# Three HGRN projections cut by halves of the heads, the query taken token-major, and the recurrence two slots earlier, in a one-core hybrid encoder block

## What is computed

```python
proj = h @ w_in[l]
(q_hg, i_hg, f_fw, f_bw, g_hg, c_q, c_kv, k_rope, q_mem, gates) = _split(proj, IN_SPLITS)

q = heads(jax.nn.silu(q_raw)); v = heads(i_raw)
f = lbz + (1.0 - lbz) * jax.nn.sigmoid(f_raw)      # forward and backward
k = heads(1.0 - f); log_f = heads(jnp.log(f))
o = _chunk_gla(qz, kz, vz, gz)                     # S_t = diag(f_t) S_{t-1} + k_t v_t^T ; o_t = S_t^T q_t
o = _rmsnorm(o[0] + flip(o[1]), norm_g) * jax.nn.sigmoid(g_raw)
```

## Time and profile before

| | us |
|---|---|
| median of 3 runs | 1706.37 (1706.21 to 1706.91) |
| the profiled execution | 1706.24 |
| its span | 1704.5 |
| PE busy | 1699.0 |
| DVE busy | 1168.3 |
| ACT busy | 815.7 |
| POOL busy | 94.1 |

### The profile page before, as it was taken

How to read it: one execution, slowest core, us unless ns; L and a number is a source line. 1 busy time by engine, 2 the same in 40 slices (tenths; PEclk the granted TensorE clock), 3 DMA queues, 4 the chain that set the end, 5 groups by cost and what they waited for, 6 DMA issues and landing times.

```text
span 1704.5 us, 20450 instructions
## 1 busy us (share of the span) xinstructions
PE 1699.0 (100%) x8694; PEld 1411.7 (83%) x8694; DVE 1168.3 (69%) x1024; ACT 815.7 (48%) x674; POOL 94.1 (6%) x87
## 2 busy tenths in 40 slices
PE   9999999999999999999999999999999999999999
PEld 8888888898888888888888888888888888888886
DVE  4854566678877655545666679888989798655445
ACT  4454445454545445444444526554554555443332
POOL 0000002222222100000000000000000000000000
PEclk9999999999999999999999999999999999999999
DMA  9676776455665687667888958778787876878553
GB/s 363 240 251 209 253 242 210 174 172 184 184 208 197 198 248 270 214 213 252 256 269 278 360 198 255 242 230 260 237 243 252 240 236 180 261 239 306 198 197 124
DMA packets 137370, 397.98 MB, mean 233 GB/s; under 512 B 22336, under 2 KB 51392, under 8 KB 122816
## 3 DMA queue, kind: packets, MB, share of 16 engines
q1 hardware_dynamic: 129568, 377.15, 66.0%
q0 software_dynamic: 2720, 10.49, 3.3%
q10 hardware_dynamic: 4992, 9.05, 1.4%
HBM read 365.06 MB, written 30.93 MB: 232 GB/s over the span
## 4 chain that ended last, share of the span: by engine, by line
PE 99%; DVE 0%; ACT 0%; issue 0%; POOL 0%; DVEq 0%; POOLq 0%
PE pair L2145 21%; PE pair L2146 21%; PE pair L2147 21%; PE pair L2417 4%; PE pair L2415 4%; PE pair L2416 4%; PE pair L2119 3%; PE side L2397 3%; PE side L2395 3%; PE side L2396 3%; PE pair L2117 1%; PE pair L2397 1%; PE pair L2396 1%; PE pair L2395 1%; PE side L2227 1%; PE pair L2129 1%
## 5 line engine op out<-in xcount | busy, mean ns | idle before, releaser
L1396 DVE TENSOR_TENSOR weight_lo<-raw,weight_hi 128x2048 fp32r<-128x2048 f32 x210 | 481.0, 2292 | 396.2 <-ACT weight_hi L974 393.6
L974 ACT ACTIVATE weight_hi<-raw 128x2048 fp32r<-128x2048 f32 x210 | 402.3, 1916 | 520.1 <-DMA raw<-in_stream 519.9
L2145 PE MATMUL pair<-weight_hi,act_both 128*128 128x512 f32 x928 | 368.5, 397 | 0.6 <-DVE weight_lo L1396 0.6
L2147 PE MATMUL pair<-weight_hi,act_both 128*128 128x512 f32 x928 | 361.6, 390 | 0.0
L2146 PE MATMUL pair<-weight_lo,act_both 128*128 128x512 f32 x928 | 361.4, 389 | 0.0
L2145 PEld LDWEIGHTS pair<-weight_hi,act_both 128*128 128x128 f32 x928 | 174.3, 188 | 37.0 <-issue 1.0
L2147 PEld LDWEIGHTS pair<-weight_hi,act_both 128*128 128x128 f32 x928 | 174.2, 188 | 36.7
L2146 PEld LDWEIGHTS pair<-weight_lo,act_both 128*128 128x128 f32 x928 | 174.3, 188 | 35.3
L1295 ACT ACTIVATE part_hi<-part_raw 128x2048 fp32r<-128x2048 f32 x60 | 113.7, 1912 | 123.6 <-DVE part_raw L1887 49.8
L1867 DVE TENSOR_TENSOR part_lo<-part_raw,part_hi 128x2048 fp32r<-128x2048 f32 x60 | 136.4, 2281 | 42.7 <-ACT part_hi L1295 42.6
L2145 PE MATMUL pair<-weight_hi,ff_both 128*128 128x512 f32 x352 | 136.9, 389 | 0.0
(11 more groups left out here) (320 smaller groups left out, 2546.4 us busy)
## 6 DMA issues: line engine op xcount, KB each, us to landing
raw<-in_stream SPq DMA_DIRECT2D x256, 1024.0 KB, 5.5
part_raw<-in_stream SPq DMA_DIRECT2D x30, 1024.0 KB, 6.9
part_raw<-in_stream POOLq DMA_DIRECT2D x10, 1024.0 KB, 10.7
scratch<-spill ACTq DMA_DIRECT2D x32, 256.0 KB, 5.1
ln_rows<-in_ln_rows SPq DMA_DIRECT2D x6, 1024.0 KB, 8.3
gate<-scratch SPq DMA_DIRECT2D x12, 512.0 KB, 6.9
ff_scratch<-ff_blocks SPq DMA_DIRECT2D x11, 512.0 KB, 6.6
ff_land<-ff_scratch SPq DMA_DIRECT2D x44, 128.0 KB, 5.5
```

The costliest lines, as they stand in the source:

```text
L974: act.activation(hi_of(n), raw_of(n), ACT.Copy).then_inc(extra_h if extra(n) else h_ready, 1)
L1396: dve.tensor_tensor(lo_of(n), raw_of(n), hi_of(n).bitcast(F32), ALU.subtract)\
L2145: pe.matmul(out, hi[:, k0 + k, tok], w_hi[:, k, :], start=first and k == 0, stop=False)
L2147: mm = pe.matmul(out, lo[:, k0 + k, tok], w_hi[:, k, :], start=False, stop=last and k == 3)
```

## The change

The pieces of `f_fw`, `f_bw` and `q_hg` are cut by halves of the heads and put in the order f_fw0, f_bw0, q_hg0, f_fw1, f_bw1, q_hg1, four pieces each, in the same 24 slots (24 to 47). The query's pieces become token-major, like the gates', with the same way through transposition, DRAM and `f_land`; silu is applied where the gates have the sigmoid. `HG_SLOT` goes from 49 to 47. All other phases keep their slots; so do the first 8 attention units, while the 4 memory units, which are counted from the end of the recurrence, come two slots earlier.

```diff
-PHASES = [("mem_k", 8), ("mem_v", 8), ("c_q", 4), ("c_kv", 4), ("f_fw", 8), ("f_bw", 8), ("q_hg", 8), ("i_hg", 8),
+PHASES = [("mem_k", 8), ("mem_v", 8), ("c_q", 4), ("c_kv", 4), ("f_fw0", 4), ("f_bw0", 4), ("q_hg0", 4),
+          ("f_fw1", 4), ("f_bw1", 4), ("q_hg1", 4), ("i_hg", 8),
...
+HG_ROWS = ("f_fw", "f_bw", "q_hg")
+HG_HALVES = [(_name, _c) for _c in range(2) for _name in HG_ROWS]
...
-SPLIT = ("mem_k", "q_hg")
+SPLIT = ("mem_k",)
...
-TURNED = [(_name, _c) for _name in ("f_fw", "f_bw", "q_mem", "g_hg") for _c in range(2)]
-TURNED_TAKEN = [FIRST[_name] + 4 * (_c + 1) for _name, _c in TURNED]
+TURNED = HG_HALVES + [(_name, _c) for _name in ("q_mem", "g_hg") for _c in range(2)]
+TURNED_TAKEN = [FIRST[f"{_name}{_c}"] + 4 for _name, _c in HG_HALVES]\
+    + [FIRST[_name] + 4 * (_c + 1) for _name, _c in TURNED[len(HG_HALVES):]]
...
-F_ROWS = 4
+F_ROWS = len(HG_HALVES)
...
-HG_SLOT, HG_STEPS, PAIRS = FIRST["i_hg"] + 1, 12, 4
+HG_SLOT, HG_STEPS, PAIRS = FIRST["i_hg"] - 1, 12, 4
...
                 if n - 6 in TURNED_TAKEN[:F_ROWS]:
                     i = TURNED_TAKEN.index(n - 6)
-                    f, c = (f_fw, f_bw)[i // 2], i % 2
+                    c, d = divmod(i, 3)
+                    to = (f_fw, f_bw, q_hg)[d]
...
-                    act.activation(squared(f[:, 4 * c:4 * c + 4, :]), slices(f_land[:, i % 2]), ACT.Sigmoid)\
-                       .then_inc(f_open, 1)
-                j = n - 1 - FIRST["q_hg"]
-                if 2 <= j <= 8 and j % 2 == 0:
-                    wait_taken(act, GROUP["q_hg"] + j // 2 - 1)
-                    act.activation(q_hg[:, j - 2:j, :], q_hg[:, j - 2:j, :], ACT.Silu).then_inc(q_open, 1)
+                    act.activation(squared(to[:, 4 * c:4 * c + 4, :]), slices(f_land[:, i % 2]),
+                                   ACT.Silu if d == 2 else ACT.Sigmoid).then_inc(f_open, 1)
...
                 if s == 0:
-                    if p == 0:
-                        dve.wait_ge(q_open, 4)
-                        dve.wait_ge(f_done, F_ROWS)
+                    if p % 2 == 0:
+                        dve.wait_ge(f_open, 3 * (p // 2 + 1))
+                        dve.wait_ge(f_done, 2 * (p // 2 + 1))
...
-                j = n - FIRST["q_hg"]
-                if 2 <= j <= 8 and j % 2 == 0:
-                    add_halves(n, GROUP["q_hg"] + j // 2 - 1, q_hg[:, j - 2:j, :])
...
-            t_phase("f_fw", 8, 4, act_hi, act_lo)
-            t_phase("f_bw", 8, 4, act_hi, act_lo)
-            f_phase("q_hg", 8, act_both)
+            for name, c in HG_HALVES:
+                t_phase(f"{name}{c}", 4, 4, act_hi, act_lo)
```

More of the change, by code:

```diff
@@ L66 @@
     PIECES += _count
-GROUPS = {"mem_k": 4, "mem_v": 2, "q_mem": 2, "g_hg": 2, "f_fw": 2, "f_bw": 2, "q_hg": 4, "i_hg": 2, "c_q": 1, "c_kv": 1,
+GROUPS = {"mem_k": 4, "mem_v": 2, "q_mem": 2, "g_hg": 2, "f_fw0": 1, "f_bw0": 1, "q_hg0": 1,
+          "f_fw1": 1, "f_bw1": 1, "q_hg1": 1, "i_hg": 2, "c_q": 1, "c_kv": 1,
           "uq_nope": 4, "uq_rope": 2, "uk": 4, "uv": 2, "k_rope": 1, "gates": 12, "branch": 12, "w_o": 4, "ffn": 2,
@@ L75 @@
     _g += GROUPS[_name]
-TWO_BY_256 = ("c_q", "c_kv", "f_fw", "f_bw", "q_mem", "g_hg", "gates", "branch", "ffn")
-SPLIT = ("mem_k", "q_hg")
+HG_ROWS = ("f_fw", "f_bw", "q_hg")
+HG_HALVES = [(_name, _c) for _c in range(2) for _name in HG_ROWS]
+TWO_BY_256 = ("c_q", "c_kv") + tuple(f"{_name}{_c}" for _name, _c in HG_HALVES)\
+    + ("q_mem", "g_hg", "gates", "branch", "ffn")
+SPLIT = ("mem_k",)
 LOW = {}
@@ L86 @@
 U_KM, U_VM, U_GATES = 0, 4, 8
-TURNED = [(_name, _c) for _name in ("f_fw", "f_bw", "q_mem", "g_hg") for _c in range(2)]
-TURNED_TAKEN = [FIRST[_name] + 4 * (_c + 1) for _name, _c in TURNED]
+TURNED = HG_HALVES + [(_name, _c) for _name in ("q_mem", "g_hg") for _c in range(2)]
+TURNED_TAKEN = [FIRST[f"{_name}{_c}"] + 4 for _name, _c in HG_HALVES]\
+    + [FIRST[_name] + 4 * (_c + 1) for _name, _c in TURNED[len(HG_HALVES):]]
+TURNED_GROUP = [GROUP[f"{_name}{_c}"] for _name, _c in HG_HALVES]\
+    + [GROUP[_name] + _c for _name, _c in TURNED[len(HG_HALVES):]]
 TURNED_SAVED = [_n + 5 for _n in TURNED_TAKEN]
 TURNED_FETCHED = [_n + 7 for _n in TURNED_TAKEN]
-F_ROWS = 4
+F_ROWS = len(HG_HALVES)
 LOOK = 2
@@ L344, in encoder_program @@
         f_open = sem("f_open")
-        q_open = sem("q_open")
         f_done = sem("f_done")
@@ L553, in columns_of_two @@
                             src = phase(name, "(c h b f) p e -> c b f p h e", h=2, b=3, f=2)[c, b, q // 2]
-                        elif name in ("f_fw", "f_bw", "q_mem", "g_hg"):
+                        elif name[:-1] in HG_ROWS:
+                            first = FIRST["f_fw0"] + 8 * HG_ROWS.index(name[:-1])
+                            src = stream[first:first + 8].rearrange("(c h f) p e -> c f p h e", h=2, f=2)
+                            src, q = src[int(name[-1]), j // 2], j
+                        elif name in ("q_mem", "g_hg"):
                             c, q = j // 4, j % 4
@@ L1103, in slot @@
                         act.wait_ge(kz_done, 1)
-                    take(n, GROUP[name] + c, rows[:], ACT.Copy, 512)
+                    take(n, TURNED_GROUP[i], rows[:], ACT.Copy, 512)
                 if n - 6 in TURNED_TAKEN[:F_ROWS]:
                     i = TURNED_TAKEN.index(n - 6)
-                    f, c = (f_fw, f_bw)[i // 2], i % 2
+                    c, d = divmod(i, 3)
+                    to = (f_fw, f_bw, q_hg)[d]
                     if i == 0:
@@ L1667, in slot @@
                     name, c = TURNED[i]
-                    wait_taken(dve, GROUP[name] + c)
+                    wait_taken(dve, TURNED_GROUP[i])
                     rows, blocks = (f_rows, f_blocks[:]) if i < F_ROWS else (qg_rows, qg_blocks[:])
@@ L1673, in slot @@
                         squares(blocks, t, rows[:, t, :], rows_blocked)
-                if n - 7 in TURNED_TAKEN[:F_ROWS]:
-                    i = TURNED_TAKEN.index(n - 7)
-                    d, c = divmod(i, 2)
+                i = TURNED_TAKEN.index(n - 7) if n - 7 in TURNED_TAKEN[:F_ROWS] else None
+                if i is not None and TURNED[i][0] != "q_hg":
+                    c, d = divmod(i, 3)
                     f = (f_fw, f_bw)[d]
```

## The result

The changed kernel takes **1712.99 us** (median of 8 runs, 1709.69 to 1714.01) against 1706.36 (median of 8, 1705.94 to 1707.20): a ratio of 1.0035 with a 95% interval of 1.0025 to 1.0044. It is slower by 6.6 us, where 1707.5 was forecast with a range of 1704.9 to 1709.1. The profiled execution is the slowest of the eight: 1714.01 us with a span of 1712.2, 7.8 us more than the one before.

A forecast was written before the change was run, and what follows sets the result against it. PE alone was taken to set the time. 1706.24 - 1.03 for the query + 2.15 for the passage gave 1707.36; with the median 0.13 higher, 1707.5 us was forecast, range 1704.9 to 1709.1.

The forecast's parts named there:

- What bounds the kernel: Whole kernel: PE alone sets the time, busy 1699.0 us of 1704.5; only PE's own work or new PE waits count.
- The query's form, -1.03: Eight query pieces: token-major form needs 64 matmuls fewer on PE, 1.03 us less, all on the path.
- the query saves nothing: Rival at the query pieces: the token-major form saves nothing, with the stall in place, 1708.5 us; chance 0.04.
- What is exchanged beside PE, 0: DVE, ACT and SP exchanges hidden by PE's 5.44 us pieces; PE's side products cost 0, between -0.3 and +0.3.
- The passage from pair 0 to pair 1, +2.15 between 1.65 and 2.55: Pieces 60 to 62: PE late for step 1 through DVE's late hg_rs reading, containing 1.05 us for piece 61's bank.
- The recorded reading of rows 7 and 8: DVE's query rotation: one of two equal multiplications took 2.06 us beside a POOL instruction, the other 1.22.
- The other passages: Slots 72 and 84: PE has more time and slot 72 no rotation, so no stall should decide there.
- The rival named 1711.8: The passage costs 2.15 us at all three pairs, slots 72 and 84 too; 0.10 with any other large stall.
- all passages or another large stall: Line of the chances: stalls at all three pair passages or some other large stall, 1711.8 us; chance 0.10.
- In most slots nothing: Recurrence two slots earlier: costs nothing in most slots, except at the passage from one pair of heads to the next.

The follow-up runs named there:

- experiment 2: Changed kernel with the recurrence put back to its old slot (49), leaving the order by halves and the token-major query: 1706.02 us against 1706.72 for the kernel before.
- experiment 6, first kernel: Changed kernel with the qm_land fetches behind loads 104 and 105 and DVE's query rotation in slot 62 instead of 60: 1706.52 us, ratio 0.9999.
- experiment 1: Changed kernel with the eight qm_land fetches put back behind weight loads 104 and 105: 1707.66 us against 1706.72 for the kernel before, ratio 1.0005.
- one copy: Changed kernel with fetches put back, rotation in slot 62, later step 1 packing, plus one unused ACT copy ahead of piece 104's split: 1706.68 us.
- experiment 6: Three kernels on the changed one with fetches put back: rotation in slot 62, 1706.52 us; step 1 packing behind k_nope's second taking (the 2.24 stall), 1708.01; both, 1705.83.
- experiment 7: Changed kernel with rotation in slot 62 and later step 1 packing, but the qm_land fetches left ahead of load 104: 1711.44 us against 1706.54 before.
- experiment 6 with both edits: Changed kernel with fetches behind loads 104 and 105, rotation in slot 62 and step 1 packing behind k_nope's second taking: 1705.83 us, ratio 0.9995.

## Why the prediction was wrong, point by point

- **What bounds the kernel.** Right: apart from the start and the 1.03 us of matmuls saved, all of the difference between the two traces is PE kept waiting or PE at a lower clock.
- **The query's form, -1.03.** Right. The first matmuls of pieces 32, 40 and 48 are now at 189.44, 232.96 and 276.48: 43.52 us for either eight, the figure that the earlier trace rows gives for the token-major ones. The rival "the query saves nothing" falls.
- **What is exchanged beside PE, 0.** Right as to DVE and ACT: experiment 2 shows no new wait beside the pieces that were exchanged; its one new wait, 0.3 us at 923.58, is far behind them.
- **The passage from pair 0 to pair 1, +2.15 between 1.65 and 2.55.** Right in place, order and size, and 0.27 too high. The timeline of DVE in the changed kernel answers to the earlier trace rows:

```profile
356.38 1.22 DVE L1493 TENSOR_TENSOR rope_x<-rope_x,cos 128x1024 f32<-128x1024 f32 x1
357.51 1.45 DVE L1494 TENSOR_TENSOR rope_swapped<-rope_swapped,sin 128x1024 f32<-128x1024 f32 x1
358.99 1.32 DVE L1496 SCALAR_TENSOR_TENSOR q_rope<-rope_swapped,small,rope_x 128x1024 f32<-128x1024 f32 x1
...
364.44 0.68 DVE L1568 TENSOR_SCALAR hg_rs<-side 128x512 f32<-128x512 f32 x1
```

  and that of PE to the earlier trace rows:

```profile
356.91 0.40 PE L2252 MATMUL side<-square_lo,ones_hi 128*128 128x512 f32 x1
357.24 0.46 PE L2232 MATMUL side<-q_hat,k_hat 128*32 128x32 f32 x32
358.70 0.50 PE L2150 MATMUL pair<-weight_hi,c_hi 128*128 128x512 f32 x1 [1.01 <-ACT k_nope L1017]
...
365.18 0.46 PE L2232 MATMUL side<-q_hat,k_hat 128*32 128x32 f32 x32 [0.72 <-DVE hg_rs L1568]
```

  With L = 357.31 the rotation begins at L - 0.93 (forecast L - 0.9), the reading ends at L + 7.81 (L + 7.6 to 8.5), piece 61 waits 1.01 (1.05), and step 1 starts at L + 7.87 instead of L + 5.99: 1.88 late. (The recorded sum is itself off by 0.05: the middle of 1.65 and 2.55 is 2.10, with a tenth for the signal 2.20.) About half of the excess is the rotation, 3.93 us (356.38 to 360.31) instead of the middle of 3.6 and 4.5, 4.05: beside POOL's copies its second operation took 1.45, where it had taken 2.06 beside POOL's multiplication. The rest is in terms of a few hundredths each, such as the signal, 0.06 and not 0.1.
  The recorded reading of rows 7 and 8 is too simple: POOL's record, 355.10 to 356.96, lies beside both multiplications nearly equally long, and only the second one is longer. What the rotation takes without POOL is shown by experiment 6, first kernel, where POOL's last copy ends as the rotation begins: 1.21, 1.22 and 1.28, 3.67 in all (forecast 3.6). Its second operation there:

```profile
370.30 1.22 DVE L1494 TENSOR_TENSOR rope_swapped<-rope_swapped,sin 128x1024 f32<-128x1024 f32 x1
```

- **The other passages.** Right that they don't decide: no wait of PE is seen at slots 72 and 84. The rival named 1711.8 for it, near the measured time, but by a mechanism that did not happen. The line of chances widens it to "all passages or another large stall" with 0.10; that is what came, but no place and no cause was named for it, so the nearness of 1711.8 to 1712.99 is luck. A number that fits is no support for its story.
- **The step that failed** is "In most slots nothing, since a product of the recurrence has a whole slot between its packing and its use". It looks at the products only. The edit moves everything that is counted from `HG_END`, and on SP that includes the eight `qm_land` fetches, past two loads that are not moved, 104 and 105; `prob_t` is queued behind the first. The prediction names SP once, for the savings that were added and their fetches, and never asks what the two slots carry past on its queue. The term that it lacked is 3.47 us in the profiled execution (experiment 1 takes away 5.3 by the medians, the clock's part included), and its danger could have been read before: 0.72 us between the end of `prob_t` and PE, behind a split that had waited 4.82 us for its load, and fetches that take SP 3.79 us to issue.
- **The second omission** is the clock. All of the sum's stalls were priced at their own length. That holds for the passage, where the stalls were short, and not behind piece 102, where 2.75 us came on top of 3.47.

With both terms, taken from the slowest execution, and the measured passage the sum by the prediction's own method would have been 1706.37 - 1.03 + 1.88 + 3.47 + 2.75 = 1713.4; measured 1712.99.

## What to carry to other kernels

When an edit changes a number that other places count from, list everything that hangs on it engine by engine, the DMA queues above all, and ask of each what it passes. Then look for the instruction that stands behind a load it doesn't need: the cover that counts is the one of the whole queue ahead of it, not of its own inputs. In this kernel, which is bound by PE, the stalls under 2 us cost what they lasted, and a stall that made PE 3.5 us late cost 6.2 in all, because of the clock.

## What the runs showed of the hardware that was not expected

- **The clock after a stall.** In work that kept PE busy throughout, stalls with the starts around them 1.46 (`k_nope` in the changed kernel), 1.86 (one copy), 2.24 (experiment 6) and 2.70 us apart (experiment 7) left the granted clock at its full level, 2.4 GHz, in the profiled execution. With starts 3.43 and 3.70 apart it went to 1.2 GHz, and PE worked at that level for 3.5 us (634.0 to 637.5) and 5.4 us (636.2 to 641.6) after it had begun again. The loss on top of the stall was 1.7 us in the first case and 2.75 in the second.
- **A price that depends on the neighbour.** The same DVE multiplication of 128x1024 with two inputs took 1.22 us with POOL idle (experiment 6, first kernel), 1.45 beside POOL's copies and 2.06 beside POOL's multiplication, while the one in front of it, beside the same multiplication for most of its time, took 1.22. Spans on POOL are rough in the profile, so why only the second pays stays open. The Trainium skill ("GPSIMD Engine Reference", section 1) says that POOL contends with such instructions of VectorE; the second multiplication agrees, the first shows none of it, and the traces add that it matters much what POOL does.
- **Small fetches ahead of a large load.** Eight fetches of 128 KB take SP 3.8 to 5.6 us to issue, and the 1 MB load behind them can't be issued sooner. From its own issue to its split that load took 9.2, 8.7 and 8.3 us in the three traces with all eight fetches ahead of it, and 7.3 to 8.6 in the nine without. A slower transfer is likely, but the ranges meet; the late issue is the sure part.
- **The start differs.** The second instruction of PE began at 7.41, 7.50 and 8.42 us in three of the kernels (experiment 6 with both edits, before and changed), whose beginnings are the same. For a difference of a microsecond between two profiled executions this has to be taken off first.
